# First-block queries, keys and values as three rounded products instead of one full-precision product

## The chip, the cores and the metric

The kernel runs on one core of one Trainium2 chip. The metric is the device time of one execution in microseconds (us), as a median of runs. Engines are called by their names: TensorE (matmul), VectorE, ScalarE, GpSimd and SyncE, whose queue issues most of the weight loads.

## The reference, cut to what matters

One transformer block with mixture of experts (first block), then two layers of a second block, on 256 tokens of width 1024. The change lies in the input projections of the first block:

```
mod = (silu(c) @ w_ada + b_ada);  mod_ctx = silu(c_ctx) @ w_ada[:, :2*d] + b_ada[:2*d]
h  = modulate(rms_norm(x, norm_mix_g), sh_mix, sc_mix)        # 256 x 1024, latents
hc = modulate(rms_norm(ctx, norm_mix_g), ...)                  # 256 x 1024, context
tq, tk, tv = h @ w_in[:, 64-wide columns]                      # "tiny" attention, tk, tv of hc too
nq = h @ w_in[:, COL_NQ:COL_NK] + b_in                         # 512 columns, latents only
nk = h, hc @ w_in[:, COL_NK:COL_NV] + b_in                     # 512 columns, latents and context
nv = h, hc @ w_in[:, COL_NV:COL_GA] + b_in                     # 512 columns, latents and context
o_b = neighbourhood_attention(nq, nk, nv, nk_c, nv_c, rpb)     # s_lat + rpb position bias, band mask -inf
```

After it come the gates, the experts and the second block. All values are float32.

## The kernel before, in words

One program, its order written out by hand on every engine. Weights go through a ring of nine slots of 128 x 2048 floats (1 MB each), loaded by SyncE in the fixed order of `plan()`; a load waits until the last job that used its slot is full (`units.before`, L722 issues it). PSUM has eight banks, dealt out in rings by `plan()`. `ring_low` is the same memory as `weight_ring`, seen as float32r.

The order on TensorE at the start (`mod_rows`, `turn_pair`, `mod_columns`, L979 to L1005) makes the modulation rows of `w_ada` and turns the normed inputs; ScalarE (L1619) and VectorE (L2027) write the modulated inputs, feature-major, to `hT` (context and latents, eight 128 x 256 tiles each). Meanwhile `keep_busy(("tiny", 0), 3)` (L967) runs three matmuls of no use. Then come:

- `tiny`: four `token_major` calls (L926) of 192 columns.
- `nq`: two `feature_major` calls (L939), 32 products of 256 columns in all.
- `nk`: four `feature_major` calls of eight products of 512 columns, with a step of the tiny attention behind each (`tiny_turns`, `tiny_scores`, `tiny_probs_turn`, `tiny_sum`; L895, L1027, L1040).
- `nv`: four `token_major` calls of eight products of 512 columns.
- the neighbourhood attention `NA_QUADS` = 8 times: scores (L1067), turns, sums (L1085), with the projections v and u as filler (L1098), and `ada_product` on VectorE (L2106, L2109).

A float32 product stands in the trace as two MATMUL records; a float32r product as one.

VectorE's order there is: the four `tiny` outputs (`biased_out`, L2039), the `nq` outputs (L2048), the rotation of the tiny queries and keys (L2068 to L2071), `keys_low` (L2078) for each `nk`, the tiny softmax (L2087 to L2094), the four `nv` outputs. GpSimd loads the position table: one DMA makes 64 copies of `na_rpb` in DRAM (`rpb_copies`, L844), as soon as the last `w_ada` unit has landed; twelve DMAs with rows of 64 floats gather it into `posb` (L850); then comes `w_sT` (L855); then GpSimd adds the band mask to all of `posb` (L860, 128 x 6144), and VectorE's attention loop waits for it (`posb_ready`).

The later weights of the first block (`upa`, `upb`, `wo`) and all of the second block are already computed as three products of rounded halves: ScalarE copies the weights to float32r (`first_high`, L1674), VectorE writes the rest, weights minus the copy, in place (`first_low`, L2166), and `token_split` (L955) or `feature_split` (L1376) takes high x high, high x low and low x high (`PASSES`).

Of the kernel before, what the change touches and what calls it, by code (L numbers as in the profile page):

```python
# [163 lines left out]
def plan():  # L164
# [36 lines left out]
    for t in range(4):  # L201
        long.take(("nv", t))
    main.take(("tqT", 0))
# [38 lines left out]

    units.at += (SLOTS - 1 - units.at) % SLOTS
# [156 lines left out]
FIRST_SPLIT = [("upa", 0, 0), ("upa", 0, 1), ("upb", 0), ("upa", 1, 0), ("upa", 1, 1), ("upb", 1),  # L400
               ("wo", 0, 0), ("wo", 0, 1), ("wo", 1, 0), ("wo", 1, 1)]
FIRST_UPPER = [20480, 24576, 10240, 22528, 12288, 24576, 20480, 10240, 22528, 12288]
# [8 lines left out]
def build(nc, a):  # L411
    banks, units, freed_by, sources, order, last_jobs = plan()
    ctx = ExitStack()
    with ctx:
# [33 lines left out]
        with nc.sbuf_tensor("below_first", [P, 10240], F32), nc.sbuf_tensor("first_upper", [P, 16384], F32R) as first_upper:  # L448
            pass
# [52 lines left out]
        nq32 = area(10240, 4, S)  # L502
# [5 lines left out]
        pr, prT = area(12288, 2, CHUNK), area(13312, 2, CHUNK)  # L508
# [119 lines left out]
        def upper(key, it):  # L628
            if key in FIRST_SPLIT:
                at = FIRST_UPPER[FIRST_SPLIT.index(key)]  # L630
                return first_upper[:, at - 10240:at - 10240 + SLOT]
            place = high_place(key, it)
            return high_ring[:, place, :] if place < 4 else high_late[:, (1, 2, 0)[place - 4], :]
# [196 lines left out]
        def _(pool):  # L830
# [60 lines left out]
        def _(pe):  # L891
# [39 lines left out]
            def feature_major(key, right, tokens, units_, fts, it=0):  # L931

                wait_bank(pe, key, it)
                for s_, f in enumerate(fts):
                    for n in range(KT):
                        uk = units_[n // 4]
                        if s_ == 0 and n % 4 == 0:
                            wait_weights(pe, uk, it)
                        last = mm(bank(key)[:, s_ * tokens:(s_ + 1) * tokens],  # L939
                                  w(uk, 4, CHUNK)[:, n % 4, f * P:(f + 1) * P], right[:, n],  # L940
                                  start=(n == 0), stop=(n == KT - 1))
                full(last, key)

            def token_split(key, left, t, units_, kts, it, between=None):

                wait_bank(pe, key, it)
                n = 0
                for uk in units_:
# [4 lines left out]
                    for j in range(kts):  # L953
                        for i, (a_, b_) in enumerate(PASSES):
                            last = mm(bank(key)[:, :], left[:, a_, n, t * P:(t + 1) * P], wv[b_][:, j, :],  # L955
                                      start=(n == 0 and i == 0), stop=(n == kts * len(units_) - 1 and i == 2))
                        n += 1
                full(last, key)
# [49 lines left out]
            keep_busy(("tiny", 0), 3)  # L1008
# [6 lines left out]
            for p in range(2):  # L1015
                feature_major(("nq", p), hT[:, 0], S, both(("win", "nq")), (2 * p, 2 * p + 1))
# [351 lines left out]
            def feature_split(key, right, units_, fts, it):  # L1368
                wait_bank(pe, key, it)
                for s_, f in enumerate(fts):  # L1370
                    for n in range(KT):
                        uk = units_[n // 4]
                        if s_ == 0 and n % 4 == 0:
                            wait_split(pe, uk, it)
                        for i, (a_, b_) in enumerate(PASSES):
                            last = mm(bank(key)[:, s_ * S:(s_ + 1) * S], halves(uk, CHUNK, it)[a_][:, n % 4, f * P:(f + 1) * P],  # L1376
                                      right[:, b_, n, :], start=(n == 0 and i == 0), stop=(n == KT - 1 and i == 2))
                full(last, key)

# [212 lines left out]
        def _(act):  # L1592
# [17 lines left out]
            for half in range(2):  # L1610
# [4 lines left out]
                for g in (2 * half, 2 * half + 1):  # L1615
# [5 lines left out]
                    out(last, ("cT", g))  # L1621
            def keys_high(f):
# [49 lines left out]
            def first_high(*key):  # L1672
                wait_weights(act, key)
                A(upper(key, 0), ring[:, units.place[key][0], :], ACT.Copy).then_inc(sem("first_high_ready"), 1)  # L1674

# [289 lines left out]
        def _(dve):  # L1965
# [78 lines left out]
            for p in range(2):  # L2044
                wait_full(dve, ("nq", p))
                for j in range(2):
                    f = 2 * p + j
                    last = V.tensor_scalar(nq32[:, f, :], bank(("nq", p))[:, j * S:(j + 1) * S], in_b[:, f:f + 1],  # L2048
                                           NDH ** -0.5, ALU.add, ALU.mult)
# [750 lines left out]
```

## Time and profile before

| | |
|---|---|
| median of 3 runs | 1685.28 us (1685.15 to 1686.44) |
| the profiled execution | 1687.72 us, its span 1685.9 us |
| TensorE busy | 97% of the span |
| VectorE, ScalarE, GpSimd busy | 49%, 34%, 2% |
| granted TensorE clock, mean | 0.988 |
| DMA | 418.53 MB, mean 248 GB/s |

The span is the time of the instructions of the profiled execution; 1.8 us of its own time lie around it. A matmul's record is longer than its share of the pipelined engine, so the pace of matmuls is read from the starts of successive groups in the timeline.

### The profile page before, as it was taken

To read this page: it belongs to the slowest core of one execution; us is meant where nothing else is said; L and a number is where in the kernel's file an instruction comes from. 1 tells how busy PE (TensorE), PEld (TensorE's weight loads), DVE (VectorE), ACT (ScalarE), POOL (GpSimd) and SP (SyncE) were. 2 spreads that over 40 slices of the span, in tenths; PEclk is the share of its full clock that TensorE was granted. 3 is DMA by queue.
4 is the path that set the end of the run, shared out by engine and by line. 5 is a ranking of instruction groups with operands and counts; after the bars stand their busy time and mean duration, and the time that the engine had idled before them with its cause. 6 is when DMAs were issued, how large, how long until landed. Compare 5 with 4: busy or idle time off the path is not lost.

```text
span 1685.9 us, 21598 instructions
## 1 busy us (share of the span) xinstructions
PE 1628.7 (97%) x9036; PEld 1131.6 (67%) x9037; DVE 823.8 (49%) x1176; ACT 581.4 (34%) x807; POOL 41.5 (2%) x49
## 2 busy tenths in 40 slices
PE   5999999999999999999998999999999999999998
PEld 3744544775444444444446877799998877799997
DVE  2128934663222222222226775874537684765454
ACT  1013431331111111111113666554434475644432
POOL 0320010000000000000000000000000000000000
PEclk9999999999999999999999999999999999999999
DMA  9935873673999999999993444465535543556440
GB/s 360 262 139 194 305 281 117 225 282 154 419 421 421 421 421 421 421 421 421 420 375 125 150 150 147 156 223 173 202 119 207 175 150 125 200 165 210 158 168 25
DMA packets 148288, 418.53 MB, mean 248 GB/s; under 512 B 6960, under 2 KB 55104, under 8 KB 123168
## 3 DMA queue, kind: packets, MB, share of 16 engines
q1 hardware_dynamic: 125904, 271.19, 44.5%
q10 hardware_dynamic: 17568, 127.93, 18.2%
q0 software_dynamic: 4720, 18.03, 3.5%
q8 instruction: 73, 1.20, 0.3%
q14 instruction: 23, 0.19, 0.0%
HBM read 416.07 MB, written 2.95 MB: 249 GB/s over the span
## 4 chain that ended last, share of the span: by engine, by line
PE 91%; DVE 5%; ACT 1%; SPq 1%; issue 1%; DMA 1%; DVEq 0%; ACTq 0%
PE bank L955 18%; PE bank L1274 13%; PE bank L1580 12%; PE bank L1285 7%; PE bank L1530 6%; PE bank L926 6%; PE bank L1256 4%; PE bank L1295 4%; PE bank L895 3%; PE bank L1098 3%; PE bank L1551 3%; PE bank L1376 3%; PE bank L939 2%; SPq L722 1%; DMA weight_ring<-in_w_ada 1%
## 5 line engine op out<-in xcount | busy, mean ns | idle before, releaser
L2429 DVE TENSOR_TENSOR ring_low<-weight_ring,high_ring 128x2048 fp32r<-128x2048 f32 x92 | 207.9, 2287 | 59.8 <-ACT high_ring L1784 59.4
L1274 PE MATMUL bank<-weight_ring,arena 128*64 128x512 f32 x800 | 232.1, 592 | 0.7 <-DVE arena L2349 0.7
L955 PE MATMUL bank<-high_ring,split 128*128 128x512 f32 x608 | 201.2, 405 | 0.0
L955 PE MATMUL bank<-ring_low,split 128*128 128x512 f32 x448 | 181.3, 405 | 0.0
L1274 PEld LDWEIGHTS bank<-weight_ring,arena 128*64 128x64 f32 x800 | 74.5, 137 | 150.2 <-issue 150.2
L1784 ACT ACTIVATE high_ring<-weight_ring 128x2048 fp32r<-128x2048 f32 x92 | 171.6, 1905 | 10.5 <-PE bank L955 5.9
L1580 PE MATMUL bank<-split,ring_low 128*128 128x256 f32 x576 | 162.6, 282 | 0.0
L1580 PE MATMUL bank<-split,high_ring 128*128 128x256 f32 x832 | 148.9, 280 | 0.0
L955 PEld LDWEIGHTS bank<-high_ring,split 128*128 128x128 f32 x608 | 117.6, 193 | 33.1 <-issue 3.4
L1580 PEld LDWEIGHTS bank<-split,high_ring 128*128 128x128 f32 x832 | 128.8, 189 | 0.7
L1285 PE MATMUL bank<-weight_ring,arena 128*64 128x512 f32 x400 | 120.5, 598 | 0.6 <-DVE arena L2349 0.6
L1274 PE MATMUL bank<-arena 128*64 128x512 f32 x256 | 112.5, 592 | 0.0
L2408 DVE SCALAR_TENSOR_TENSOR arena<-bank,cols,arena 128x256 f32<-128x256 f32 x33 | 16.0, 484 | 193.1 <-ACT arena L1752 193.1
L1580 PEld LDWEIGHTS bank<-split,ring_low 128*128 128x128 f32 x576 | 108.8, 189 | 0.0
L2423 DVE TENSOR_TENSOR split<-bank,split 128x512 fp32r<-128x512 f32 x66 | 45.6, 691 | 125.9 <-ACT split L1766 125.9
L955 PEld LDWEIGHTS bank<-ring_low,split 128*128 128x128 f32 x448 | 86.2, 192 | 17.8
L926 PE MATMUL bank<-weight_ring,arena 128*128 128x512 f32 (+1 forms) x256 | 94.0, 526 | 0.0
L1766 ACT ACTIVATE split<-bank 128x512 fp32r<-128x512 f32 x66 | 39.4, 597 | 146.0 <-PE bank L1285 146.0
L1256 PEld LDWEIGHTS bank<-routed 128*128 128x128 f32 x544 | 66.7, 190 | 27.4 <-issue 27.4
L1752 ACT ACTIVATE arena<-bank 128x256 f32<-128x256 f32 x33 | 12.7, 384 | 209.0 <-PE bank L1274 209.0
L895 PE MATMUL bank<-const,arena 128*128 128x128 f32 (+1 forms) x530 | 76.0, 282 | 6.8 <-DVE arena L2690 3.0
L1285 PEld LDWEIGHTS bank<-weight_ring,arena 128*64 128x64 f32 x400 | 34.4, 136 | 68.7 <-issue 68.7
(309 smaller groups left out, 2663.5 us busy)
## 6 DMA issues: line engine op xcount, KB each, us to landing
weight_ring<-in_w_in SPq DMA_DIRECT2D x62, 1024.0 KB, 8.1
weight_ring<-in_w_e_gate SPq DMA_DIRECT2D x49, 1024.0 KB, 9.1
weight_ring<-in_w_e_up ACTq DMA_DIRECT2D x46, 1024.0 KB, 14.4
weight_ring<-in_w_e_down ACTq DMA_DIRECT2D x46, 1024.0 KB, 14.2
weight_ring<-in_w_ada SPq DMA_DIRECT2D x24, 1024.0 KB, 13.7
weight_ring<-in_w_ffn_gate SPq DMA_DIRECT2D x22, 1024.0 KB, 5.5
weight_ring<-in_w_ffn_up SPq DMA_DIRECT2D x22, 1024.0 KB, 8.0
weight_ring<-in_w_ffn_down SPq DMA_DIRECT2D x22, 1024.0 KB, 5.5
```

The source lines that it names most:

```text
L895: return nc.tensor.transpose(dst, src, k("ident")[0:m, 0:m])
L926: last = mm(bank(key)[:, 0:cols_], left[:, n, t * P:(t + 1) * P], wv[:, j, :], start=(n == 0), stop=(n == kts * len(units_) - 1))
L955: last = mm(bank(key)[:, :], left[:, a_, n, t * P:(t + 1) * P], wv[b_][:, j, :], start=(n == 0 and i == 0), stop=(n == kts * len(units_) - ...
L1098: last = mm(bank((name, n, t))[:, :], hT[:, 0, kt, t * P:(t + 1) * P], w(weights, 4, CHUNK)[:, kt % 4, :], start=(kt == 0), stop=(kt == KT ...
L1256: last = mm(down_banks[j][:, s_ * QUAD * CAP:s_ * QUAD * CAP + n], h2s[:, part, t, kt, :], onehot[:, q % 2, t, 0:n], start=(t == 0 and par ...
L1274: last = mm(hidden_bank[side * CAP:(side + 1) * CAP, :].rearrange("p (j n) -> p j n", n=FF), xgT[:, p // 2 % 2, kt, at:at + CAP], hidden_u ...
L1285: last = mm(down_banks[n][side * CAP:(side + 1) * CAP, :], hidT[:, p % 2, at:at + CAP], down_unit(e % DOWN_UNITS)[:, f, n * CHUNK:(n + 1) ...
L1295: last = mm(y_bank(n, t)[:, :], sent[:, p % 3, t * P:(t + 1) * P], ys[:, part, n * CHUNK:(n + 1) * CHUNK], start=False, stop=(p == PAIRS a ...
L1530: last = mm(bank(key)[:, :], fh[:, (2 * d + f) % 4, a_, t * P:(t + 1) * P], wv[b_][:, f, n * CHUNK:(n + 1) * CHUNK], start=(d == 0 and f = ...
L1580: last = mm(bank(key)[:, j * S:(j + 1) * S], wv[a_][:, kt, f * P:(f + 1) * P], xs[:, b_, kt, :], start=(kt == 0 and i == 0), stop=(kt == K ...
L1784: A(upper(key, layer), ring[:, units.place[key][0], :], ACT.Copy).then_inc(sem("high_ready"), 1)
L2429: V.tensor_tensor(lower(key), ring[:, units.place[key][0], :], upper(key, layer), ALU.subtract)\
```

## The change

The six weight units of `nq`, `nk` and `nv` are added to `FIRST_SPLIT`, and the inputs are split as well: `hup` (float32r copies of `hT`, by ScalarE) and `hl` (the rest, by VectorE). The upper halves of the weights need room: three of them lie in the ring's slots 6, 7 and 8, which therefore count as used until `nk` and `nv` are done, and the order in which the ring's slots are dealt out is permuted until the gates are through. `keep_busy` ahead of `tiny` goes. The gather of the position table waits for the last `nv` weights to land, `w_sT` for `nq_low`; the mask is added by VectorE in two halves. Tiles that stood in the new buffers' place move (`nq32`, `pr`, `prT`).

```diff
+    units.owner[6] = units.owner[7] = ("win", "nk", 1)
+    units.owner[8] = ("win", "nv", 1)
+    units.slots, units.at = [0, 1, 2, 3, 6, 7, 4, 5, 8], 0
...
+    units.slots = list(range(SLOTS))
     units.at += (SLOTS - 1 - units.at) % SLOTS
...
+FIRST_SPLIT = [("win", name, half) for name in ("nq", "nk", "nv") for half in range(2)]
+FIRST_SPLIT += [("upa", 0, 0), ("upa", 0, 1), ("upb", 0), ("upa", 1, 0), ("upa", 1, 1), ("upb", 1),
...
+FIRST_UPPER = [18432, 14336, 6, 7, 8, 28416, 20480, 24576, 10240, 22528, 12288, 24576, 20480, 10240, 22528, 12288]
...
+        hup = input_split[:, 2048:6144].rearrange("p (w k t) -> p w k t", w=2, k=KT)
+        hl = [input_split[:, at:at + KT * S].rearrange("p (k t) -> p k t", k=KT) for at in (16896, 0)]
...
@@ GpSimd
             pool.wait_ge(sem("copies_stored"), 16)
+
+            wait_weights(pool, ("win", "nv", 1))
             for half in range(2):
...
+            pool.wait_ge(sem("nq_low"), 1)
             pool.dma_start(wsT, a["w_sT"]).then_inc(sem("sgu_landed"), 16)
-
-            pool.wait_ge(sem("const_landed"), 16)
-            pool.wait_ge(sem("posb_landed"), 16 * 2 * DR)
-            flat = posb.rearrange("p h r c -> p (h r) c")
-            nc.gpsimd.tensor_tensor(flat, flat, k("window").unsqueeze(1).to_broadcast([P, NH * DR, GRID_W]),
-                                    ALU.add).then_inc(sem("posb_ready"), 1)
...
@@ TensorE
-            keep_busy(("tiny", 0), 3)
...
             for p in range(2):
-                feature_major(("nq", p), hT[:, 0], S, both(("win", "nq")), (2 * p, 2 * p + 1))
+                if p == 0:
+                    pe.wait_ge(sem("input_low"), 1)
+                feature_split(("nq", p), (hup[:, 0], hl[0]), both(("win", "nq")), (2 * p, 2 * p + 1), 0)
+
+            def keys_split(f):
+
+                wait_bank(pe, ("nk", f))
+                for n in range(KT):
+                    uk = ("win", "nk", n // 4)
+                    if f == 0 and n % 4 == 0:
+                        wait_split(pe, uk, 0)
+                    high_, low_ = [v[:, n % 4, f * P:(f + 1) * P] for v in halves(uk, CHUNK, 0)]
+                    mm(bank(("nk", f))[:, :], high_, hup[:, :, n, :], start=(n == 0), stop=False)
+                    for j in range(2):
+                        mm(bank(("nk", f))[:, j * S:(j + 1) * S], high_, hl[j][:, n, :], start=False, stop=False)
+                    last = mm(bank(("nk", f))[:, :], low_, hup[:, :, n, :], start=False, stop=(n == KT - 1))
+                full(last, ("nk", f))
...
             for f, tiny_step in enumerate((tiny_turns, tiny_scores, tiny_probs_turn, tiny_sum)):
-                feature_major(("nk", f), hT.rearrange("p w k t -> p k w t"), 2 * S, both(("win", "nk")), (f,))
+                if f == 0:
+                    pe.wait_ge(sem("input_low"), 2)
+                keys_split(f)
                 tiny_step()
             for t in range(4):
-                token_major(("nv", t), hT[:, t // 2], t % 2, both(("win", "nv")), 4)
+                token_split(("nv", t), (hup[:, t // 2], hl[t // 2]), t % 2, both(("win", "nv")), 4, 0)
...
@@ ScalarE
+            wait_out(act, ("xT", 3))
+            A(hup[:, 0], hT[:, 0], ACT.Copy).then_inc(sem("input_high"), 1)
+            wait_out(act, ("cT", 3))
+            A(hup[:, 1], hT[:, 1], ACT.Copy).then_inc(sem("input_high"), 1)
+            first_high("win", "nq", 0)
+            first_high("win", "nq", 1)
+            for half in range(2):
+                wait_full(act, ("ar", SHIFT_SCALE[3]))
+                first_high("win", "nk", half)
+            wait_full(act, ("tiny", 3))
+            first_high("win", "nv", 0)
+
+            act.wait_ge(sem("tiny_roped"), 1)
+            first_high("win", "nv", 1)
...
@@ VectorE
-            for t in range(4):
+            def tiny_out(t):
                 lo = 0 if t < TT else TINY
                 biased_out(("tiny", t), tqkv[:, t, lo:], 3 * TINY, lo)
+
+            dve.wait_ge(sem("input_high"), 1)
+            V.tensor_tensor(hl[0], hT[:, 0], hup[:, 0], ALU.subtract).then_inc(sem("input_low"), 1)
+            first_low("win", "nq", 0)
+            tiny_out(0)
+            first_low("win", "nq", 1)
+            tiny_out(1)
+
+            for t in range(TT):
...
+            last.then_inc(sem("tiny_roped"), 1)
+            tiny_out(2)
+            first_low("win", "nk", 0)
+            tiny_out(3)
+
+            dve.wait_ge(sem("input_high"), 2)
+            V.tensor_tensor(hl[1], hT[:, 1], hup[:, 1], ALU.subtract).then_inc(sem("input_low"), 1)
+            first_low("win", "nk", 1)
+            first_low("win", "nv", 0)
             for p in range(2):
                 wait_full(dve, ("nq", p))
...
+            first_low("win", "nv", 1)
+
...
             keys_low(3)
+            flat = posb.rearrange("p h r c -> p (h r) c")
+            n_rows = NH * DR // 2
             for t in range(4):
+                if t < 2:
+
+                    if t == 0:
+                        dve.wait_ge(sem("posb_landed"), 16 * 2 * DR)
+                    part = flat[:, t * n_rows:(t + 1) * n_rows, :]
+                    V.tensor_tensor(part, part, k("window").unsqueeze(1).to_broadcast([P, n_rows, GRID_W]), ALU.add)\
+                        .then_inc(sem("posb_ready"), 1)
                 biased_out(("nv", t), nv[:, t, :])
```

## Rows read from the trace of the kernel before

**Rows 1.** The page: busy time by engine; chain that ended last, by engine.

```profile
PE 1628.7 (97%) x9036; PEld 1131.6 (67%) x9037; DVE 823.8 (49%) x1176; ACT 581.4 (34%) x807; POOL 41.5 (2%) x49
PE 91%; DVE 5%; ACT 1%; SPq 1%; issue 1%; DMA 1%; DVEq 0%; ACTq 0%
```

**Rows 2.** Timeline of TensorE, 40 to 131 us: start us, us, engine, line, operation.

```profile
40.20 5.29 PE L967 MATMUL bank<-const 128*128 128x512 f32 x6
45.33 10.56 PE L926 MATMUL bank<-weight_ring,arena 128*128 128x192 f32 x64
55.73 20.84 PE L939 MATMUL bank<-arena,weight_ring 128*128 128x256 f32 x80
77.06 7.03 PE L939 MATMUL bank<-arena,weight_ring 128*128 128x512 f32 x16
84.03 1.98 PE L1027 MATMUL bank<-arena 64*128 64x512 f32 x4
...
102.81 27.73 PE L926 MATMUL bank<-weight_ring,arena 128*128 128x512 f32 x64
131.85 0.98 PE L1067 MATMUL bank<-split 32*128 32x512 f32 x12 [1.30 <-DVE arena L2039]
```

**Rows 3.** Timeline of TensorE, rounded products: 512 columns at 312 us, 256 at 916.

```profile
312.55 0.40 PE L955 MATMUL bank<-first_upper,split 128*128 128x512 f32 x1
...
318.15 0.40 PE L955 MATMUL bank<-first_upper,routed 128*128 128x512 f32 x1
...
916.66 0.40 PE L1376 MATMUL bank<-split,high_ring 128*128 128x256 f32 x2
...
919.85 0.40 PE L1376 MATMUL bank<-split,high_ring 128*128 128x256 f32 x2
```

**Rows 4.** Busy time by stretch, with PEclk, the granted TensorE clock, DMA share, GB/s.

```profile
20.00:30.00 10.00, 10.00 (x72) 7.32 (x72) 0.70 (x5) 1.32 (x3) 0.00 (x0) 1.00 1.05 387
...
40.00:45.00 5.00, 5.00 (x8) 2.36 (x9) 2.48 (x8) 1.93 (x4) 0.00 (x0) 0.50 0.97 355
45.00:50.00 5.00, 5.00 (x30) 4.67 (x29) 0.36 (x1) 0.00 (x0) 3.64 (x5) 0.98 1.00 309
...
460.00:600.00 140.00, 140.00 (x716) 66.76 (x713) 36.21 (x84) 23.42 (x46) 0.00 (x0) 1.00 1.01 421
```

**Rows 5.** Timeline of ScalarE and VectorE at the end of `hT`.

```profile
41.05 1.93 ACT L1619 ACTIVATE arena<-bank,cols 128x256 f32<-128x256 f32 x4 [3.57 <-DVE cols L2020]
...
41.05 1.90 DVE L2027 TENSOR_SCALAR arena<-bank,cols 128x256 f32<-128x256 f32 x4
```

**Rows 6.** Instructions of `first_upper`: the two halves of a weight unit, ns min/median/max.

```profile
L1674 ACT ACTIVATE first_upper<-weight_ring x10: 1893/1912/1917, 273.5 to 338.4; 128x2048 fp32r<-128x2048 f32 x10
L2166 DVE TENSOR_TENSOR ring_low<-weight_ring,first_upper x10: 2281/2284/2285, 287.4 to 342.4; 128x2048 fp32r<-128x2048 f32 x10
```

**Rows 7.** SyncE's issues of `nk` unit 1 and `nv` unit 0; each one's time to landing.

```profile
34.78 1.07 SPq L722 DMA_DIRECT2D weight_ring<-in_w_in  x1
...
weight_ring<-in_w_in SPq DMA_DIRECT2D x1, 1024.0 KB, 34.9
...
35.89 9.34 SPq L722 DMA_DIRECT2D weight_ring<-in_w_in  x1
...
weight_ring<-in_w_in SPq DMA_DIRECT2D x1, 1024.0 KB, 43.1
```

**Rows 8.** SyncE's issue of `nq` unit 0, to landing; DMA queues, 46.4 to 78.7 us.

```profile
25.86 5.21 SPq L722 DMA_DIRECT2D weight_ring<-in_w_in  x1
...
weight_ring<-in_w_in SPq DMA_DIRECT2D x1, 1024.0 KB, 20.4
...
q0 software_dynamic: 1094, 3.64, 53.8%
q1 hardware_dynamic: 2016, 4.00, 49.3%
```

**Rows 9.** Timeline of GpSimd: gather of the table, mask.

```profile
46.36 9.74 POOL L850 DMA_DIRECT2D arena<-rpb_copies  x12 [10.69 <-DMA rpb_copies<-in_na_rpb]
...
78.68 13.85 POOL L860 TENSOR_TENSOR arena<-arena,const 128x6144 f32<-128x6144 f32 x1 [22.03 <-DMA arena<-rpb_copies]
```

**Rows 10.** Timeline of VectorE: outputs, rotation, subtraction of 1024 columns, tiny softmax.

```profile
48.30 0.36 DVE L2039 TENSOR_TENSOR arena<-bank,arena 128x192 f32<-128x192 f32 x1 [5.34 <-PE bank L926]
...
69.74 0.88 DVE L2048 TENSOR_SCALAR arena<-bank,cols 128x256 f32<-128x256 f32 x2 [6.03 <-PE bank L939]
...
70.77 0.90 DVE L2068 TENSOR_TENSOR arena<-arena,const 128x32 f32<-128x32 f32 x8
...
78.27 1.22 DVE L2083 TENSOR_TENSOR split<-arena,split 128x1024 fp32r<-128x1024 f32 x1 [0.19 <-ACT split L1628]
...
87.43 5.38 DVE L2094 TENSOR_SCALAR arena<-arena,cols 128x512 f32<-128x512 f32 x1
...
92.92 0.49 DVE L2094 TENSOR_SCALAR arena<-arena,cols 128x512 f32<-128x512 f32 x1
...
130.59 0.69 DVE L2039 TENSOR_TENSOR arena<-bank,arena 128x512 f32<-128x512 f32 x1 [6.18 <-PE bank L926]
```

More of the change, by code:

```diff
@@ L929, in token_major @@
                 full(last, key)
[L931 to L942, printed above, removed]
             def token_split(key, left, t, units_, kts, it, between=None):
+                if not isinstance(left, tuple):
+                    left = left[:, 0], left[:, 1]
                 wait_bank(pe, key, it)
@@ L954, in token_split, with feature_split @@
                         for i, (a_, b_) in enumerate(PASSES):
-                            last = mm(bank(key)[:, :], left[:, a_, n, t * P:(t + 1) * P], wv[b_][:, j, :],
+                            last = mm(bank(key)[:, :], left[a_][:, n, t * P:(t + 1) * P], wv[b_][:, j, :],
                                       start=(n == 0 and i == 0), stop=(n == kts * len(units_) - 1 and i == 2))
                         n += 1
+                full(last, key)
+            def feature_split(key, right, units_, fts, it):
+                if not isinstance(right, tuple):
+                    right = right[:, 0], right[:, 1]
+                wait_bank(pe, key, it)
+                for s_, f in enumerate(fts):
+                    for n in range(KT):
+                        uk = units_[n // 4]
+                        if s_ == 0 and n % 4 == 0:
+                            wait_split(pe, uk, it)
+                        for i, (a_, b_) in enumerate(PASSES):
+                            last = mm(bank(key)[:, s_ * S:(s_ + 1) * S], halves(uk, CHUNK, it)[a_][:, n % 4, f * P:(f + 1) * P],
+                                      right[b_][:, n, :], start=(n == 0 and i == 0), stop=(n == KT - 1 and i == 2))
                 full(last, key)
@@ L1015, in _ @@
             for p in range(2):
-                feature_major(("nq", p), hT[:, 0], S, both(("win", "nq")), (2 * p, 2 * p + 1))
+                if p == 0:
[3 more added lines that the diff above has]
+                wait_bank(pe, ("nk", f))
+                for n in range(KT):
+                    uk = ("win", "nk", n // 4)
[7 more added lines that the diff above has]
+                full(last, ("nk", f))
             def tiny_turns():
@@ L1366, in _ @@
             overflow(pe, most, products)
[L1368 to L1378, printed above, removed]
             for layer in range(L2):
@@ L1621, in _, with first_high @@
                     out(last, ("cT", g))
+            def first_high(*key):
+                wait_weights(act, key)
+                A(upper(key, 0), ring[:, units.place[key][0], :], ACT.Copy).then_inc(sem("first_high_ready"), 1)
+            wait_out(act, ("xT", 3))
[11 more added lines that the diff above has]
+            first_high("win", "nv", 1)
             def keys_high(f):
@@ L2039, in biased_out, with first_low @@
                 out(V.tensor_tensor(dst, bank(key)[:, lo:n], bias[:, i % 2, lo:n], ALU.add), key)
-            for t in range(4):
+            def first_low(*key):
+                dve.wait_ge(sem("first_high_ready"), FIRST_SPLIT.index(key) + 1)
+                V.tensor_tensor(lower(key), ring[:, units.place[key][0], :], upper(key, 0), ALU.subtract)\
+                    .then_inc(sem("first_split_ready"), 1)
+            def tiny_out(t):
                 lo = 0 if t < TT else TINY
                 biased_out(("tiny", t), tqkv[:, t, lo:], 3 * TINY, lo)
[L2044 to L2049, printed above, removed]
-                    if j == 0:
-                        step(last)
-                out(last, ("nq", p))
-                wait_out(dve, ("nq", p))
-                dve.sem_inc(sem("nq_ready"), 1)
+            dve.wait_ge(sem("input_high"), 1)
[4 more added lines that the diff above has]
+            tiny_out(1)
             for t in range(TT):
@@ L2075, in _ @@
             last.then_inc(sem("tiny_roped"), 1)
+            tiny_out(2)
[5 more added lines that the diff above has]
+            first_low("win", "nv", 0)
+            for p in range(2):
+                wait_full(dve, ("nq", p))
+                for j in range(2):
+                    f = 2 * p + j
+                    last = V.tensor_scalar(nq32[:, f, :], bank(("nq", p))[:, j * S:(j + 1) * S], in_b[:, f:f + 1],
+                                           NDH ** -0.5, ALU.add, ALU.mult)
+                    if j == 0:
+                        step(last)
+                out(last, ("nq", p))
+                wait_out(dve, ("nq", p))
+                dve.sem_inc(sem("nq_ready"), 1)
+            first_low("win", "nv", 1)
             def keys_low(f):
```

21 lines of the change are left out of this document (7 added, 14 removed).

## The prediction

> **What bounds the kernel now.** I read the page first: TensorE is busy for 97% of the span, and it holds 91% of the chain that ended last [rows 1]. So a microsecond of TensorE work saved is worth a microsecond unless a new wait takes it. Next comes TensorE's timeline around the change [rows 2]. From 45.33 to 130.5 us the engine goes from one product to the next without a gap: tiny, `nq`, `nk`, `nv`. The one idle stretch is 1.30 us ahead of the first attention scores, which wait for VectorE's output of the last `nv`. DMA, VectorE and ScalarE are all off this path. I then looked for what would be on it afterwards: when `hT` is complete [rows 5], what a split costs [rows 6], when the weights land [rows 7, 8], and what GpSimd and VectorE do meanwhile [rows 9, 10].
>
> **The change part by part.**
>
> *Products.* A full float32 product of 512 columns costs (84.03 - 77.06) / 8 = 0.871 us [rows 2]. Of the 20.84 us group, one `nk` call of 6.97 goes off, which leaves 13.87 us for the 32 products of `nq`. A rounded product of 512 columns costs (318.15 - 312.55) / 24 = 0.233 us, and one of 256 columns (919.85 - 916.66) / 27 = 0.118 us [rows 3].
> - `nq`: 96 x 0.118 = 11.3 us for 13.9. Gain 2.5.
> - `nk`: `keys_split` takes two of 512 and two of 256 columns for each k, 2 x 0.233 + 2 x 0.118 = 0.703 us; 32 of them are 22.5 us for 4 x 6.97 = 27.9. Gain 5.4.
> - `nv`: 96 x 0.233 = 22.4 us for 27.7 [rows 2]. Gain 5.3.
>
> Together 13.2 us. That a high half is loaded three times running in `keys_split` is not charged: rows 3 hold one weight load for each 256-column product already.
>
> *Start of tiny.* `hT` is done at 41.05 + 1.93 = 43.0 us [rows 5], so without the useless matmuls tiny may begin there and not at 45.33. But the clock is at half (1.2 GHz) from 40 to 45 us and at 2.4 from then on [rows 2, 4]: L967 needed 5.1 us of full-width matmuls before it rose, and now the engine stands still from 40.3 to 43.0 instead. Tiny takes 10.4 us at the full clock. If the clock rises at 45.2 as now, tiny ends at 45.2 + 10.4 - 1.1 = 54.5, which is 1.2 earlier than 55.7. If it stays at half for all of tiny, it ends at 43.0 + 20.8 = 63.8, 8.1 later. I take L967's own 5.1 us, the nearest row: half clock to 48.1, 2.55 us worth of work done, the end at 48.1 + 7.85 = 56.0, a loss of 0.3. The Trainium skill (TensorE: Matmul & The Clock Gate, Part 1) has the throttled state as the default, which only sustained activity releases; that speaks against dropping the warm-up, and by it the clock would still be at half when tiny begins. The late bound stays in the range because rows 4 show half clock in a stretch where the engine was busy throughout.
>
> *Splits ahead of `nq` and `nk`.* A high half costs ScalarE 1.91 us, a low half VectorE 2.28 [rows 6]; the inputs have the same 2048 columns. ScalarE: `hup` of the latents 43.0 to 44.9, of the context to 46.8. `nq` unit 0 lands at 25.86 + 20.4 = 46.3 [rows 8], so its high half ends at 48.7. Unit 1 I put at 49.7 (its high half at 51.6), and the later units at intervals of 2.7 us (1 MB at 387 GB/s, rows 4) behind it: 52.4, 55.1, 57.8, 60.5. High halves: `nk` 54.3 and 57.0, `nv` 59.7 and 62.4. VectorE: `hl` 47.2, `nq` unit 0 51.0, a tiny output (0.36, rows 10), unit 1 53.9, output, the rotation (2 x 1.3 us, rows 10) to 57.0, output, `nk` unit 0 59.7, output, the context's `hl` 62.3, `nk` unit 1 64.6, `nv` unit 0 66.9, `nq` outputs (0.9 each, the second not before `nq` is full), `nv` unit 1 by 71. TensorE wants `nq` at 56.0, `nk` at 67.3 and its unit 1 at 70.1, `nv` at about 95. Each is ready 2 to 24 us before. Cost on the path: none; the tightest covers are tiny for `nq` unit 1 (2.1 us) and `nq` for the context's input (5).
>
> *Weights and the gather.* Those landings need the moved gather. Now `nk` unit 1 lands at 34.78 + 34.9 = 69.7 and `nv` unit 0 at 79.0 [rows 7], since in 46.4 to 78.7 us the gather's queue holds 53.8% of the DMA engines and the weights' 49.3% [rows 8]. Behind `nv` unit 1 the gather leaves them the engines. Its own packets took 0.538 x 32.3 = 17.4 us of all engines, so it would land 17 to 32 us after 60.5, at 78 to 93; `w_sT` and the biases queue behind it on GpSimd and are wanted after 118. On SyncE's queue the loads of `v` now wait for `nq` to be full (67) and `w_ada`'s for `nk` (94); they are wanted at 119 and 124. No cost.
>
> *Mask.* GpSimd's 13.85 us [rows 9] become two adds of 3072 columns on VectorE. From 1.22 us for 1024 and 2.28 for 2048 [rows 6, 10] I get 3.35 us each. The first starts behind `keys_low(3)` at about 94 (table landed by 93) and ends at 97.5; the first `nv` is full at 101, the second add runs 101.7 to 105.1, and the second `nv` is full at 106.5. Hidden; the four banks of `nv` are free anyway. VectorE also loses a drag: its L2094 took 5.38 us while GpSimd ran the mask, 0.49 right behind it [rows 9, 10]; nobody on the path waited, so nothing is counted. The 1.30 us stall behind the last `nv` [rows 2, 10] stays.
>
> *Downstream.* Attention begins 13.2 - 0.3 = 12.9 us earlier with the same work. In the expert stage TensorE is busy for 140.00 of 140.00 us, with DMA at 421 GB/s [rows 4]; both start later or earlier with the slots that the same matmuls free, so the shift passes. The slots' order is back to what it was at `upa`.
>
> **Sum.** The profiled execution has a span of 1685.9 and 1687.7 in all; 12.9 less is 1673.0 and 1674.8. The median of the runs shown, 1685.28, lies 2.4 below that execution, and it gives 1672.4 us.
>
> **The rivals.**
> 1. *The splits hold TensorE* (a wait takes the place of the matmuls saved). If weights go on landing as now: `nk` unit 1 at 69.7, its high half 71.6, its low half 73.9, where TensorE wants it at 70.1: 3.8 us. VectorE is an ordered queue, and behind it `nv` unit 0 (79.0, low half at 83.2) holds the `nq` outputs and so `nqs` and the turned tiny keys on ScalarE, until about 87, where TensorE wants the tiny scores at 84: some 3 more. Gain 6, 1679.2. For it: the 2.1 us cover and a chain of 25 us across two engines. Against: rows 8 say who holds the DMA engines.
> 2. *Slower than before: the table comes too late.* VectorE's wait for the gather stands ahead of all four `nv` outputs. Attention starts 3.35 + 0.69 + 3.35 + 3 x 0.69 + 1.3 = 10.8 us after the landing; it starts at 131.85 now, so the change is slower only if the gather lands after 121, 60 us behind the last weights. A landing at 128, for instance, gives 1692. Now it needs 32 us beside an equal stream of weights [rows 8, 9]: unlikely.
> 3. *The gain is swallowed later* (the change does what it says, the time stays). DMA moves 421 GB/s with no free share in the expert stage [rows 4]; if its stream did not start earlier, the end of that stage would stand still: 1685.3. Against: every load of it waits for a slot freed on TensorE.
> 4. *Half clock through tiny*: tiny ends 8.1 late, nothing later gives that back, gain 13.2 - 8.1 = 5.1: 1680.2. For it: rows 4 show a busy engine at half clock. Against: the clock rose behind 5.1 us of full-width matmuls.
>
> **How the numbers follow.** Forecast 0.70; rival 1 0.12; rival 4 0.06 (both still faster); rival 3 0.07; rival 2 0.05. Low end: clock up at once (1.2 more than a loss of 0.3: 1.5) and one later short stretch of half clock that falls away (2): 1672.4 - 3.5 = 1669. High end: rivals 1 and 4, 1680. What is left out is rivals 2 and 3 and a little. A measurement here tells about 0.2%, 3.4 us: faster 0.88, same 0.07, slower 0.05.
>
> **What would show it.** Right: L926 of 192 columns starts at 43; L1376's group at about 56, the `nk` products at 67; four `nv` calls of 5.6 us; first L1067 at 119; L2166's six new rows with no TensorE idle behind them; the table landed before 94. Wrong: idle time of TensorE at `nq` or `nk` released by VectorE, PEclk at 0.5 beyond 50 us, a VectorE wait for `rpb_copies` past 101, or a first L1067 at 119 with an end that has not moved as far.

## The result, and the profile after

The changed kernel takes 1671.56 us (median of 4 runs, 1670.86 to 1672.41), the kernel before 1685.86 in the same series (1685.15 to 1687.48). The ratio is 0.9914, with a 95% interval of 0.9901 to 0.9926: 14.3 us faster. The forecast was 1672.4. The profiled execution took 1671.87 us with a span of 1670.1; the kernel before had 1685.9.

TensorE's timeline over the same stretch as [rows 2]; the lines have new numbers (`tiny` L936, `nq` L969, `nk` L1040 to L1043, `nv` L954, attention scores L1098):

```profile
40.71 13.49 PE L936 MATMUL bank<-weight_ring,arena 128*128 128x192 f32 x64 [3.08 <-ACT arena L1638]
53.91 0.53 PE L969 MATMUL bank<-input_split,first_upper 128*128 128x256 f32 x2
...
65.41 0.40 PE L1040 MATMUL bank<-input_split,ring_low 128*128 128x512 f32 x1
...
71.03 0.82 PE L905 MATMUL bank<-const,arena 128*64 128x128 f32 x6
...
93.53 3.05 PE L954 MATMUL bank<-ring_low,input_split 128*128 128x512 f32 x12
...
117.37 0.98 PE L1098 MATMUL bank<-split 32*128 32x512 f32 x12 [1.30 <-DVE arena L2073]
```

From 40.71 to 116 us TensorE has no idle time: no split, weight or table is waited for. `nq` takes 11.50 us, the first `nk` product 5.62 (71.03 - 65.41), and the 1.30 us stall ahead of the attention is the old one. VectorE, ScalarE and GpSimd beside it:

```profile
38.35 1.93 ACT L1638 ACTIVATE arena<-bank,cols 128x256 f32<-128x256 f32 x4 [1.93 <-DVE cols L2054]
...
51.18 2.29 DVE L2077 TENSOR_TENSOR ring_low<-weight_ring,first_upper 128x2048 fp32r<-128x2048 f32 x1 [0.57 <-ACT first_upper L1643]
...
61.00 4.48 DVE L2077 TENSOR_TENSOR ring_low<-weight_ring,ring_low 128x2048 fp32r<-128x2048 f32 x2
...
93.14 3.35 DVE L2162 TENSOR_TENSOR arena<-arena,const 128x3072 f32<-128x3072 f32 x1
99.39 0.69 DVE L2073 TENSOR_TENSOR arena<-bank,arena 128x512 f32<-128x512 f32 x1 [2.91 <-PE bank L954]
...
60.91 9.77 POOL L864 DMA_DIRECT2D arena<-rpb_copies  x12 [25.45 <-DMA weight_ring<-in_w_in]
```

The first line is ScalarE's end of `hT`, 40.28 us, against 42.98 in [rows 5]. The low half of `nq` unit 1 is ready at 53.47, 0.4 us before TensorE asks for the first `nq` product and 2 us before it asks for this unit; `nk` unit 1 is ready at 63.3 and wanted at 68.2. Neither mask add of 3.35 us waits for the table. SyncE's issues of `nk` unit 1 and `nv` unit 0, each with its time to landing, answer [rows 7]:

```profile
34.59 1.07 SPq L734 DMA_DIRECT2D weight_ring<-in_w_in  x1
weight_ring<-in_w_in SPq DMA_DIRECT2D x1, 1024.0 KB, 20.0
...
35.71 9.76 SPq L734 DMA_DIRECT2D weight_ring<-in_w_in  x1
weight_ring<-in_w_in SPq DMA_DIRECT2D x1, 1024.0 KB, 21.6
```

They land at 54.6 and 57.3, not at 69.7 and 79.0.

**Where the 15.8 us between the two spans went.** Each term is a difference of starts in the two timelines; only the start of `nk` before, 69.60, is worked out (55.73 + 13.87, by the prediction's 13.87 us for `nq`).

| stretch | before | after | gain |
|---|---|---|---|
| start to `hT` ready | 42.98 | 40.28 | 2.70 |
| `hT` ready to the first `nq` product | 12.75 | 13.63 | -0.88 |
| `nq` | 13.87 | 11.50 | 2.37 |
| `nk` with the tiny attention's steps | 33.21 | 28.12 | 5.09 |
| `nv` and the stall to the first score | 29.04 | 23.84 | 5.20 |
| first score to the end | 1554.05 | 1552.73 | 1.32 |

The three product rows are 12.7 us. The first row isn't the change: up to there both programs do the same work in the same order, only the ring's slots are dealt out differently. In the 14 executions profiled for this study (one for each kernel) ScalarE's last group of `hT` begins either between 38.3 and 39.2 us (the changed kernel, and seven others below) or between 40.6 and 41.1 (the kernel before, and the rest), with and without the change. What differs is when TensorE's clock stands at half among the small matmuls of the modulation. The granted clock (the number before the last two) between 35 and 40 us, before and after:

```profile
35.00:40.00 5.00, 5.00 (x24) 3.34 (x24) 0.00 (x0) 0.60 (x1) 0.53 (x1) 0.50 1.10 397
35.00:40.00 5.00, 2.63 (x24) 1.86 (x16) 2.23 (x8) 2.25 (x5) 0.45 (x1) 0.97 1.09 390
```

The last row is of the same kind: between 300 and 306 us (end of gating, first products of `upa`) the granted clock is 0.72 on the mean in the trace of before, and 1.00 in the matching 284 to 290 us of the changed kernel.

### The profile page after: what moved, and what is told of

It is laid out like the page before. It is cut to its first block, busy times and chain, and to the rows that moved or that the text cites. A ratio compares the mean times of both kernels' runs of the same rounds, so it can differ in the third digit from the quotient of the medians.

```text
span 1670.1 us, 21858 instructions
## 1 busy us (share of the span) xinstructions
PE 1609.1 (96%) x9158; PEld 1141.3 (68%) x9159; DVE 842.9 (50%) x1186; ACT 596.6 (36%) x815; POOL 27.7 (2%) x48
## 4 chain that ended last, share of the span: by engine, by line
PE 89%; DVE 5%; ACT 2%; SPq 1%; issue 1%; DMA 1%; DVEq 0%; ACTq 0%
PE bank L954 19%; PE bank L1305 14%; PE bank L1599 12%; PE bank L1316 7%; PE bank L1549 6%; PE bank L1287 4%; PE bank L936 4%; PE bank L1326 4%; PE bank L969 3%; PE bank L905 3%; PE bank L1129 3%; PE bank L1570 3%; SPq L734 1%; DVE ring_low L2490 1%; DMA weight_ring<-in_w_ada 1%
## 5 line engine op out<-in xcount | busy, mean ns | idle before, releaser
L954 PE MATMUL bank<-high_ring,split 128*128 128x512 f32 x608 | 199.1, 401 | 0.2 <-DVE split L2497 0.2
L954 PE MATMUL bank<-ring_low,split 128*128 128x512 f32 x448 | 180.2, 402 | 0.0
L954 PEld LDWEIGHTS bank<-high_ring,split 128*128 128x128 f32 x608 | 116.3, 191 | 32.9 <-issue 3.4
L954 PEld LDWEIGHTS bank<-ring_low,split 128*128 128x128 f32 x448 | 85.5, 191 | 17.5
L1786 ACT ACTIVATE arena<-bank 128x256 f32<-128x256 f32 x33 | 12.7, 384 | 209.0 <-PE bank L1305 209.0
L2781 DVE TENSOR_TENSOR arena<-arena,bank 128x256 f32<-128x256 f32 x44 | 18.5, 420 | 122.0 <-ACT arena L1961 122.0
```

The lines of the kernel that those rows point to most:

```text
L954: last = mm(bank(key)[:, :], left[a_][:, n, t * P:(t + 1) * P], wv[b_][:, j, :], start=(n == 0 and i == 0), stop=(n == kts * len(units_) - ...
```

## The experiments

Each was compared with the kernel before on its own chip. The kernel before scatters more there than in the first series (1681.6 to 1691.1 in 29 runs on one chip, 1681.3 to 1692.5 over all four), so differences under 2 us are not read from one median. Ratios set against that of the changed kernel, 0.9914, are turned to microseconds with 1686.

### The products alone

`i_all_full` takes the splits out and puts the full-precision calls back, the rest of the change stays. All splits of these inputs and weights go, of which the lines below show three; TensorE also waits for the last two `tiny` outputs ahead of `tiny_turns`.

```diff
-                feature_split(("nq", p), (hup[:, 0], hl[0]), both(("win", "nq")), (2 * p, 2 * p + 1), 0)
+                feature_major(("nq", p), hT[:, 0], S, both(("win", "nq")), (2 * p, 2 * p + 1))
...
-                keys_split(f)
+                feature_major(("nk", f), hT.rearrange("p w k t -> p k w t"), 2 * S, both(("win", "nk")), (f,))
...
-                token_split(("nv", t), (hup[:, t // 2], hl[t // 2]), t % 2, both(("win", "nv")), 4, 0)
+                token_major(("nv", t), hT[:, t // 2], t % 2, both(("win", "nv")), 4)
...
-            first_high("win", "nq", 0)
-            first_high("win", "nq", 1)
...
-            first_low("win", "nq", 0)
```

> The changed kernel with every product of nq, nk and nv back in full precision, so without the splits of inputs and weights; all else of the change stays (no keep_busy ahead of tiny, gather and w_sT later, mask on VectorE, the slots' order). Theory: the rounded products are worth 13.2 us and the rest next to nothing, so this run lands 13.2 above the changed kernel, near 1684.8 us, within 1.5 of the kernel before, and the first attention score starts 13 us later than in the changed kernel. Rival: a good part of the gain comes from what moved (gather, mask, keep_busy); then it stays below 1681.

Measured: 1684.48 us, ratio 0.9996 (0.9986 to 1.0006), 13.8 us above the changed kernel by the ratios (12.9 by the medians). With full-precision products the moved gather, the mask on VectorE, the slots' order and the missing warm-up together are worth nothing that can be measured. The rival falls. In its trace the first score comes 89.1 us after `hT` (40.77 to 129.89), for 77.1 in the changed kernel: the traced difference is 12.0 us, less than the timed one.

`h_nq_split` puts the three rounded products back for `nq` alone.

> As i_all_full, but nq as three rounded products; nk and nv in full precision. Theory: 96 x 0.118 us for 13.9 us, 2.5 us below i_all_full, near 1682.3, and 10.7 above the changed kernel (nk 5.4, nv 5.3). Rival: the splits ahead of nq hold TensorE, since tiny is their only cover; then nq starts later than in i_all_full and the run is level with it or above.

Measured: 1682.26 us, ratio 0.9982 (0.9972 to 0.9992): 2.4 us below `i_all_full`, where 2.5 was expected, and 11.5 above the changed kernel, where 10.7 was. The two intervals overlap, so the times alone don't settle it; in its trace `nq` takes 11.51 us (56.14 to 67.65), as in the changed kernel. Tiny does cover the splits ahead of `nq`; its trace shows no idle TensorE there.

`c_nv_two` leaves the third product out of `nv` (the low half of the inputs by the high half of the weights), and nothing else:

```diff
-                token_split(("nv", t), (hup[:, t // 2], hl[t // 2]), t % 2, both(("win", "nv")), 4, 0)
+                token_split(("nv", t), (hup[:, t // 2], hl[t // 2]), t % 2, both(("win", "nv")), 4, 0, passes=PASSES[:2])
```

> The changed kernel with nv as two of its three products: high x high and high x low; the third, the low half of the inputs by the high half of the weights, is left out. The splits, loads and orders stay. Theory (TensorE alone sets the stretch, all else is cover): 32 products of 0.233 us less, 7.5 us, attention 7.5 us earlier: 1664 for 1671.5. Rival: the cover is used up; VectorE's two mask adds of 3.35 us lie between the nv outputs, which then come every 3.7 us, or the table's landing at 87 us; then less than 6 of the 7.5 us arrive.

Measured: 1663.36 us, ratio 0.9858 (0.9840 to 0.9876), 8.2 us below the changed kernel by the medians, 9.4 by the ratios. Its timeline has the first score at

```profile
110.59 0.97 PE L1098 MATMUL bank<-split 32*128 32x512 f32 x12 [1.30 <-DVE arena L2073]
```

with `hT` ready at 40.98: 69.6 us between the two, for 77.1 in the changed kernel. That is 7.5, the expected sum, with the same stall. Even with a third fewer products in `nv`, TensorE alone sets this stretch.

### The weights' landing

`b_gather_early` lets the gather go where it went before:

```diff
             pool.wait_ge(sem("copies_stored"), 16)
-
-            wait_weights(pool, ("win", "nv", 1))
             for half in range(2):
```

> The changed kernel with the gather of the position table where it was, behind its copies in DRAM and not behind the last nv weights. Theory: the weights land as in the kernel before (nk unit 1 at 69.7 us, nv unit 0 at 79, nv unit 1 at 82), the low half of nk unit 1 is ready at 74 where TensorE wants it at 68, and VectorE's queue behind holds the nq outputs until about 85: 6 to 9 us slower than the changed kernel, 1678 to 1681, with idle TensorE in nk released by VectorE. Rival: the moved gather is worth nothing, since the splits have slack enough; then it is level, 1671.6.

Measured: 1681.57 us, ratio 0.9978 (0.9968 to 0.9989): 10.8 us above the changed kernel by the ratios. That one line holds three quarters of the gain, where 6 to 9 us were expected. ScalarE's copies of the late weights and TensorE's waits, from its timelines:

```profile
55.40 1.92 ACT L1642 ACTIVATE ring_low<-weight_ring 128x2048 fp32r<-128x2048 f32 x1 [4.16 <-DMA weight_ring<-in_w_in]
68.49 1.92 ACT L1642 ACTIVATE ring_low<-weight_ring 128x2048 fp32r<-128x2048 f32 x1 [11.17 <-DMA weight_ring<-in_w_in]
76.65 1.91 ACT L1642 ACTIVATE ring_low<-weight_ring 128x2048 fp32r<-128x2048 f32 x1 [6.25 <-DMA weight_ring<-in_w_in]
...
72.78 0.80 PE L1039 MATMUL bank<-input_split,ring_low 128*128 128x512 f32 x1 [2.05 <-DVE ring_low L2076]
84.70 1.95 PE L1055 MATMUL bank<-arena 64*128 64x512 f32 x4 [1.05 <-ACT arena L1667]
```

The mechanism is the expected one: `nk` unit 1 lands at 68.5, its low half is ready at 72.7, and TensorE stands idle for it; ScalarE's queue, held by `nv` unit 1, holds the tiny keys and so the scores. But the idle time is only 3.1 us, less than expected, and the whole loss is more. Half clock behind the wait adds 1.6: the second half of the first `nk` product takes 4.42 us (72.78 to 77.20) for 2.81 in the changed kernel (68.22 to 71.03). So the first score comes 81.9 us after `hT` (42.73 to 124.63), 4.8 later than in the changed kernel.

`b2_early_freed` keeps the early gather and frees the two queues: the `nq` outputs before `nk` unit 1's low half on VectorE, the `nv` halves behind the tiny keys' copies on both engines.

```diff
@@ VectorE
-            first_low("win", "nk", 1)
-            first_low("win", "nv", 0)
             for p in range(2):
                 wait_full(dve, ("nq", p))
...
-            first_low("win", "nv", 1)
+            first_low("win", "nk", 1)
...
             V.tensor_tensor(nqs[:, 1], nq32, nqs[:, 0], ALU.subtract).then_inc(sem("nq_low"), 1)
+            first_low("win", "nv", 0)
+            first_low("win", "nv", 1)
```

> b_gather_early with its two ordered queues freed: VectorE writes the nq outputs before the low half of nk unit 1, and the nv halves on both engines come behind the copies of the turned tiny keys, so that weights that land late hold only the products that use them. Theory: b_gather_early's trace has 2.05 us of idle TensorE at nk (unit 1's low half, at 72.7) and 1.05 at the tiny scores (ScalarE's queue, held by nv unit 1 until 81.8); the second goes, the first stays: about 1 us faster than b_gather_early, 1680 to 1681. Rival: most of its 10 us came through the queues, in runs where they were held longer than in the profiled one; then 1676 or below.

Measured: 1678.35 us, ratio 0.9963 (0.9951 to 0.9975): 2.5 us below `b_gather_early` by the ratios, where 1 was expected (the intervals overlap, so the excess isn't shown), and above the 1676 of the rival. The wait at the tiny scores is gone. Its profiled execution happened to have `hT` ready at 40.4 us, where that of `b_gather_early` had it at 42.7, and it shows what an early start does to the wait:

```profile
74.21 0.80 PE L1039 MATMUL bank<-input_split,ring_low 128*128 128x512 f32 x1 [6.71 <-DVE ring_low L2075]
```

The landing of `nk` unit 1 doesn't come sooner when TensorE does: ScalarE's copy of it starts at 69.92 us here and at 68.49 in `b_gather_early`. TensorE wants the unit 3.2 us earlier here (2.4 from `hT`, the rest from a faster `tiny`) and gets it 1.4 later, so it waits 6.71 us, not 2.05, and loses its lead. The long idle time costs clock too: the granted clock between 70 and 78 us is 0.62 on the mean here, 0.79 in `b_gather_early`.

```profile
70.00:78.00 8.00, 3.79 (x12) 3.31 (x13) 2.29 (x1) 1.83 (x1) 0.00 (x0) 0.62 1.04 233
```

That line counts from the left: busy time of TensorE, its weight load, VectorE, ScalarE and GpSimd, then clock, DMA share and GB/s. The first score comes at 124.6 us in `b_gather_early` and at 125.6 here, however early `hT` was, for 117.4 in the changed kernel: 7.3 and 8.2 us. The timed losses are 10.8 and 8.3. The 8.3 fits; of the 10.8 some 3 us are in no trace (the profiled execution of `b_gather_early` was the fastest of its 12), and their cause is open.

### The table's landing

Three kernels hold the gather back further, until a later product is full:

```diff
-            wait_weights(pool, ("win", "nv", 1))
+            wait_full(pool, ("nk", 1))        # f_gather_nk1;  ("nk", 3), ("nv", 0) in the others
```

> The changed kernel with the gather of the position table held back further, until the second nk product is full (77 us in its trace, where it now issues at 60.9). The gather took 26.4 us there (first issue 60.9, last landing 87.3), so the table lands at about 104. Theory (the price of a late table is landing + 10.8 us, against the first attention score at 117.4): 104 + 10.8 = 114.6, still hidden, level with the changed kernel, 1671 to 1672; VectorE's first mask add starts at 104. Rival: nv's banks fill up while VectorE waits, or the add collides with the outputs; then 2 us or more slower.

> The changed kernel with the gather held back until the last nk product is full (91.3 us in its trace). Theory: landing at 117.7 without company, up to 6 later beside the four w_ada units that SyncE issues at the same moment; attention starts 10.8 us after the landing, at 128.5 to 134.5, so 11 to 17 us above the changed kernel, plus 1.7 for each stretch of half clock that the idle TensorE brings: 1682 to 1690. Rival: the wait is hidden by later slack; then under 1678.

> The changed kernel with the gather held back until the first nv product is full (99 us in its trace). Theory: landing at 125 to 131, past the 121 us that the prediction named as the point from which the late table makes the change a loss; attention starts at 136 to 142 against 131.85 in the kernel before: slower than the kernel before by 3 to 12 us, 1689 to 1698. Rival: the point lies elsewhere and the run stays below 1685.5.

VectorE's first mask add and the first attention score in each, in that order:

```profile
104.24 3.36 DVE L2162 TENSOR_TENSOR arena<-arena,const 128x3072 f32<-128x3072 f32 x1 [8.76 <-DMA arena<-rpb_copies]
119.62 0.97 PE L1098 MATMUL bank<-split 32*128 32x512 f32 x12 [1.30 <-DVE arena L2073]
```

```profile
125.03 3.36 DVE L2162 TENSOR_TENSOR arena<-arena,const 128x3072 f32<-128x3072 f32 x1 [29.55 <-DMA arena<-rpb_copies]
134.65 1.65 PE L1098 MATMUL bank<-split 32*128 32x512 f32 x12 [16.32 <-DVE arena L2073]
```

```profile
128.87 3.36 DVE L2162 TENSOR_TENSOR arena<-arena,const 128x3072 f32<-128x3072 f32 x1 [35.95 <-DMA arena<-rpb_copies]
138.50 1.65 PE L1098 MATMUL bank<-split 32*128 32x512 f32 x12 [22.72 <-DVE arena L2073]
```

| kernel | table landed | landing to first score | us (ratio to before, interval) |
|---|---|---|---|
| `f_gather_nk1` | 104.2 | 15.4, not bound by it | 1671.31 (0.9913, 0.9895 to 0.9930) |
| `f_gather_nk3` | 125.0 | 9.6 | 1688.82 (1.0015, 1.0002 to 1.0028) |
| `f_gather_nv0` | 128.9 | 9.6 | 1693.49 (1.0041, 1.0027 to 1.0056) |

VectorE waits 8.76 us for the table in `f_gather_nk1` and it costs nothing. In the other two the cover is gone. A straight line through their ratios crosses 1 at a landing of 122.8 us (the interval of `f_gather_nk3` alone allows about 121 to 125); the prediction had put the point from which the change is a loss at 121. The price after a landing is 9.6 us and not 10.8: the last output had been counted twice, once by itself and once in the 1.3 us stall, and the operations follow each other 0.1 us closer than their lengths. Set against that, TensorE comes out of the idle stretch at half clock: the first scores take 1.65 us and not 0.98, and from the first score to the end the traces have 1554.8 and 1554.9 us, for 1552.7 in `f_gather_nk1`. That is 2 us, and the same for both landings. Beyond it a microsecond of landing costs about one: the first score moves by 3.85 us for 3.84 of landing, the medians by 4.7.

### The mask, and the warm-up

`e_mask_gpsimd` gives the mask back to GpSimd, as one operation of 128 x 6144 behind the moved gather.

> The changed kernel with the mask added by GpSimd again, in one operation behind the moved gather. Theory: the table lands at 87, GpSimd needs 13.9 us, ready at 101, 16 us ahead of the attention; VectorE's adds were hidden and so is GpSimd's: level, within 1 us of the changed kernel (1671.6). Rival: the mask's move to VectorE is worth time, since GpSimd's operation slows VectorE's next to it (5.38 us for 0.49 in the kernel before); then the outputs of nv come late and the run is 2 to 5 us slower.

Measured: 1672.68 us, ratio 0.9919 (0.9904 to 0.9935), level. GpSimd's operation runs from 87.9 to 101.3, the first score comes at 117.88 with `hT` ready at 41.1, 0.3 us closer than in the changed kernel. The mask's move saves nothing. This run doesn't test the drag: the tiny softmax is through at 82.6, and the VectorE operations that run beside GpSimd's take 0.75 and 0.69 us, as elsewhere.

Three kernels ask what `keep_busy(("tiny", 0), n)` is worth: the changed kernel with n = 3 and n = 1, and the kernel before without it.

> The changed kernel with the three useless matmuls put back ahead of tiny. Theory: they cost TensorE about 5.2 us at half clock from the end of the modulation columns, against 3 us of idle time there, so tiny starts 2.2 later, but at the full clock, and needs 10.4 us instead of 13.2: level within 1 us, 1671 to 1673. Rival: the clock does not rise any sooner with them, then the run is 2 us slower, 1674; or the splits have used them as cover, then tiny's end moves nothing.

> The changed kernel with one useless matmul ahead of tiny, 1.7 us at half clock inside the 3 us that TensorE stands idle there: it delays nothing and is meant to raise the clock sooner. Theory: with three of them the run was level; with one, tiny starts on time and the clock rises at most 1.7 us earlier, a gain of 0 to 1 us: 1670.5 to 1671.5. Rival: the clock's rise is bound to when the full-width matmuls begin; then the whole 1 us or more arrives.

> The kernel before without the three useless matmuls ahead of tiny, nothing else. Theory: hT is ready 2.35 us before they end, and what tiny gains by starting earlier it loses at half clock (13.2 us for 10.4 in the changed kernel's trace): level with the kernel before, within 1 us. Rival: they are a net gain in the kernel before, and the change lost that; then this run is 2 us or more slower.

Measured: 1670.02 us, ratio 0.9912 (0.9897 to 0.9926), for three; 1671.36, ratio 0.9905 (0.9888 to 0.9921), for one; 1685.39, ratio 0.9993 (0.9979 to 1.0006), for the kernel before without it. All level. Tiny in the first two, and its row in the third:

```profile
45.38 10.64 PE L936 MATMUL bank<-weight_ring,arena 128*128 128x192 f32 x64
```

```profile
40.71 12.53 PE L936 MATMUL bank<-weight_ring,arena 128*128 128x192 f32 x64 [1.40 <-ACT arena L1639]
```

```profile
41.20 12.82 PE L926 MATMUL bank<-weight_ring,arena 128*128 128x192 f32 x64 [3.26 <-ACT arena L1618]
```

With three, tiny starts late and runs at the full clock; with none, it starts at once and runs part of its way at half. With one, tiny is 1.0 us shorter in its trace than the changed kernel's 13.49, but that isn't shown to be the matmul's doing: `b2_early_freed`, without any, has 12.53 too. From `hT` to the first `nq` product the three traces with useless matmuls (`before`, `a_keep3`, `a_keep1`) have 12.7 to 12.8 us, the eleven without have 12.7 to 13.6. So the warm-up may be worth some tenths of a microsecond, too little for the timed runs to tell. None of the variants beats the changed kernel by more than the measurement.

## Why the prediction was right

**What bounds.** Right: TensorE alone. `c_nv_two` showed it most sharply, with 7.5 of 7.5 us in its trace.

**The products.** Forecast 2.5, 5.4 and 5.3 us; the two traces give 2.4, 5.1 and 5.2. The paces read from the later stages held (11.5 us for 96 products of 256 columns, where 11.3 was forecast; 5.62 us for an `nk` product where 22.5 / 4 was forecast), and loading the same high half three times costs nothing. What is missing, 0.3 us at `nk`, lies around the tiny attention's steps between the products: 28.12 - 4 x 5.62 = 5.6 us for 33.21 - 4 x 6.97 = 5.3.

**The start of tiny.** Forecast: 13.0 us from `hT` to the first `nq` product, a loss of 0.3. Measured 13.63, a loss of 0.88. The term was small and its sign right. What it left out is the 0.43 us from `hT` (40.28) to the start of tiny (40.71), and half clock lasted longer than the 5.1 us taken: the granted clock is 0.50 until 46.5, 5.8 us after tiny's start. The 5.1 us was a loose measure: in the kernel before the clock had stood at half since 35 us, with TensorE busy. The late bound, half clock through all of tiny (rival 4), didn't occur in any trace.

```profile
40.00:45.00 5.00, 4.29 (x13) 4.32 (x14) 2.54 (x2) 3.98 (x3) 0.00 (x0) 0.50 0.98 371
45.00:50.00 5.00, 5.00 (x28) 5.00 (x28) 1.95 (x1) 2.68 (x2) 0.00 (x0) 0.85 1.03 351
```

The rule of the Trainium skill quoted there (TensorE: Matmul & The Clock Gate, Part 1: throttled is the default, activity releases it) agrees with these rows. It doesn't make the warm-up worth keeping: what tiny loses at half clock it gains by starting at once, all but 0.5 us (`k_before_nokeep`, 13.27 for 12.75 from `hT` to `nq`) to 0.9 us, and the timed runs are level.

**Splits ahead of `nq` and `nk`.** Right in the times that hang on the weights: the landings (54.6 and 57.3 for 55.1 and 57.8) and the ends of the halves (`nq` unit 1 at 53.5 for 53.9, `nk` unit 1 at 63.3 for 64.6). The cover for `nq` was thinner than computed, since `hT` came 2.7 us early and the weights didn't: `nq` unit 1 was ready 0.4 us before the start of `nq`, for 2.1 computed, and 2.0 before its own first product, for 3.5 by the same times. It held. `nk` unit 1 had 4.9 us, for 5.5.

**The moved gather.** Right that the forecast rests on it, and rival 1 named the way in which it would fail. Its size was wrong: a price of 6.8 us, all of it idle time, where `b_gather_early` costs 10.8. The term for `nk` unit 1 took the time at which TensorE wants the unit from one execution (3.8 us of wait) and counted no clock. The traces show 2.05 us of wait after a late start and 6.71 after an early one, with 1.6 and 2.2 us of half clock behind them. The second term, some 3 us at the tiny scores, was 1.05. With the changed kernel's early start the whole comes to 7.3 to 8.2; the remaining 3 us of the 10.8 stay open.

**Mask.** 3.35 us forecast for 3072 columns, 3.35 measured, hidden as said; by `e_mask_gpsimd` the move is worth nothing. That the drag in the kernel before cost nothing rests on the rows of before alone.

**Rival 2.** The same mechanism and nearly the same point, 122.8 us for 121, with two terms off in opposite directions: 1.2 us too much behind the landing, and no half clock (2 us). The example, 1692 for a landing at 128, is near `f_gather_nv0`, 1693.5 for 128.9.

**Rival 3 and downstream.** It fell: the shift of 14.5 us at the first score is 15.8 at the end (2.7 us of both are the earlier `hT`). In the expert stage the traffic stays at 421 GB/s and begins earlier: three expert weights that SyncE issued from 407.2 us on are issued from 391.2 on.

```profile
460.00:600.00 140.00, 140.00 (x722) 67.52 (x719) 35.75 (x81) 24.02 (x47) 0.00 (x0) 1.00 1.01 421
```

**The sum.** 12.9 us forecast. The stretches that the change touches gave 11.8 (12.66 - 0.88); the timed runs gave 14.3 with an interval of 12.5 to 16.7, and `i_all_full` against the changed kernel 13.8. The traced 11.8, and the 12.0 between the traces of `i_all_full` and the changed kernel, lie below the timed gain and just outside its interval. The early clock and the later half-clock stretches move that much from one execution to the next (2.70 and 1.32 us in the table), but that they make up the 1 to 2.5 us in the medians isn't shown. So the forecast of 1672.4, 0.8 from the measured 1671.56, is closer than its terms earned: with 11.8 in place of 12.9, the same base of 1685.28 would have given 1673.5.

## What to carry to other kernels

Where one engine has no idle time, price its work by the pace of the same instruction elsewhere in the trace and list every cover with its slack: here the forecast ends of the halves came true to 1.3 us. A transfer off the path can be the condition of the whole gain: one wait on GpSimd decides here between 14 us and 4. When you price a wait on something that doesn't come sooner when the waiting engine does, as a landing is, take it from the earliest start of the waiting engine that occurs, and add the clock that idle TensorE loses.

## What the runs showed of the hardware

- Fourteen kernels with the same work up to `hT` reach its end in two clusters (last ScalarE group at 38.3 to 39.2 or at 40.6 to 41.1 us), by where the half-clock stretches fall among small matmuls: with a granted clock of 0.90 to 1.00 between 35 and 38 us the group begins at 38.3 to 38.8, with 0.75 to 0.82 at 39.0 to 39.2, with 0.50 to 0.55 at 40.6 to 41.1. In the two main traces that is 2.7 of the 15.8 us between them.
- Behind 16 and 23 us of idle TensorE the clock was at half (0.50 between 130 and 140 us in `f_gather_nk3` and in `f_gather_nv0`), and the first twelve score matmuls took 1.65 us for 0.98.
- Twelve gathers with rows of 256 bytes, 3 MB in all, took 26.4 us (60.9 to 87.3) with 72.8% of the DMA engines' time on their queue (`w_sT` and a bias are on it too) and the `v` weights beside them, 32 us beside an equal stream before [rows 8, 9], and at the old place held one 1 MB weight unit back by 14 us (68.5 for 54.6).

```profile
q0 software_dynamic: 1106, 3.70, 72.8%
q1 hardware_dynamic: 693, 1.39, 24.3%
```
